# A gated linear recurrence on one Trainium2 core: keys and values of a head turned to tokens by VectorE instead of TensorE

## The reference

```python
def _gla_chunk(S, inp):
    q, k, v, logf = inp
    b = jnp.cumsum(logf, axis=2)
    ...                      # o: scores inside the chunk times v, plus q * exp(b) times S
    b_last = b[:, :, -1]
    S_new = jnp.exp(b_last)[..., None] * S + jnp.einsum(
        'bhck,bhcv->bhkv', k * jnp.exp(b_last[:, :, None] - b), v)
    return S_new, o
```

## Time and profile before

| | |
|---|---|
| median of 3 runs | 2688.05 us (2688.02 to 2688.28) |
| the profiled execution | 2687.86 us, span 2686.0 us |
| mean granted clock of TensorE | 0.998 of full |
| busy: TensorE, VectorE, ScalarE, POOL | 2656.1, 1764.7, 1300.7, 407.1 us |
| the recurrence's fourteen full trips | 440.63 us of the span |

### The profile page before, as it was taken

How to read it: one execution, slowest core, us unless ns; L and a number is a source line. 1 busy time by engine, 2 the same in 40 slices (tenths; PEclk the granted TensorE clock), 3 DMA queues, 4 the chain that set the end, 5 groups by cost and what they waited for, 6 DMA issues and landing times.

```text
span 2686.0 us, 55267 instructions
## 1 busy us (share of the span) xinstructions
PE 2656.1 (99%) x19742; PEld 2634.8 (98%) x19742; DVE 1764.7 (66%) x2908; ACT 1300.7 (48%) x2173; POOL 407.1 (15%) x792
## 2 busy tenths in 40 slices
PE   9999999999999999999999999999999999999997
PEld 9999999999999999999999999999999999999997
DVE  7888888848776534676645855548767535767644
ACT  6565666545444433444444566545444333444443
POOL 2111111101322100222200000002222101222200
PEclk9999999999999999999999999999999999999999
DMA  6444444444545555545555422344554555444553
GB/s 237 144 139 138 142 139 131 140 166 133 178 159 167 161 164 166 168 161 167 160 169 164 145 89 87 118 162 140 168 167 161 163 164 168 164 166 162 161 170 114
DMA packets 122673, 413.60 MB, mean 154 GB/s; under 512 B 13856, under 2 KB 20160, under 8 KB 122592
## 3 DMA queue, kind: packets, MB, share of 16 engines
q1 hardware_dynamic: 114480, 406.37, 47.0%
q10 hardware_dynamic: 7056, 3.21, 0.4%
q0 software_dynamic: 1056, 2.92, 0.3%
HBM read 406.97 MB, written 5.48 MB: 154 GB/s over the span
## 4 chain that ended last, share of the span: by engine, by line
PE 95%; DVE 4%; ACT 0%; issue 0%; DMA 0%; DVEq 0%; SPq 0%; ACTq 0%
PE bank L248 30%; PE bank L250 30%; PE bank L249 29%; DVE X L1163 1%; DVE Y L1160 1%; DVE h_lo L1147 1%; DVE w_lo L242 1%; PE bank L1718 1%; PE bank L828 1%; PE bank L789 1%; DVE Y L1177 1%; PE bank L796 0%; PE bank L829 0%; PE bank L1723 0%; ACT w_hi L235 0%
## 5 line engine op out<-in xcount | busy, mean ns | idle before, releaser
L248 PE MATMUL bank<-h_hi,w_hi 128*128 128x288 f32 (+1 forms) x4208 | 1262.1, 300 | 11.3 <-DVE h_lo L1147 8.4
L242 DVE TENSOR_TENSOR w_lo<-raw,w_hi 128x1024 fp32r<-128x1024 f32 (+1 forms) x784 | 952.3, 1225 | 451.8 <-ACT w_hi L235 451.4
L249 PE MATMUL bank<-h_lo,w_hi 128*128 128x288 f32 (+1 forms) x4208 | 1248.3, 297 | 0.0
L250 PE MATMUL bank<-h_hi,w_lo 128*128 128x288 f32 (+1 forms) x4208 | 1244.7, 296 | 0.0
L235 ACT ACTIVATE w_hi<-raw 128x1024 fp32r<-128x1024 f32 (+1 forms) x784 | 805.9, 1037 | 848.9 <-PE bank L250 843.0
L248 PEld LDWEIGHTS bank<-h_hi,w_hi 128*128 128x128 f32 x4208 | 788.8, 187 | 18.1 <-DVE h_lo L1147 11.4
L250 PEld LDWEIGHTS bank<-h_hi,w_lo 128*128 128x128 f32 x4208 | 792.3, 188 | 0.2
L249 PEld LDWEIGHTS bank<-h_lo,w_hi 128*128 128x128 f32 x4208 | 790.3, 188 | 0.6
L1332 POOL TENSOR_TENSOR ext<-yt,small 128x256 f32<-128x256 f32 x176 | 213.4, 1213 | 1500.8 <-ACT yt L1218 1034.7
L248 PE MATMUL bank<-g_hi,w_hi 128*128 128x288 f32 x1408 | 416.8, 296 | 0.0
L249 PE MATMUL bank<-g_lo,w_hi 128*128 128x288 f32 x1408 | 415.4, 295 | 0.0
(11 more groups left out here) (261 smaller groups left out, 2089.1 us busy)
## 6 DMA issues: line engine op xcount, KB each, us to landing
raw<-in_w_fi SPq DMA_DIRECT2D x352, 512.0 KB, 4.0
raw<-in_w_hi_in SPq DMA_DIRECT2D x128, 512.0 KB, 4.0
raw<-in_w_fo SPq DMA_DIRECT2D x128, 512.0 KB, 3.5
raw<-in_w_fo SPq DMA_DIRECT2D x64, 384.0 KB, 3.3
raw<-in_w_ho SPq DMA_DIRECT2D x32, 512.0 KB, 4.1
raw<-in_w_mo SPq DMA_DIRECT2D x32, 512.0 KB, 3.9
raw<-in_w_down SPq DMA_DIRECT2D x18, 512.0 KB, 4.1
raw<-in_w_ukv SPq DMA_DIRECT2D x16, 512.0 KB, 3.7
```

Of the source, the lines that this page charges most:

```text
L242: dve.tensor_tensor(lo, raw[:, ch.slot, 0:ch.units * P], hi.bitcast(F32), ALU.subtract).then_inc(lo_done, 1)
L248: pe.matmul(out, top[:, w], rhs_hi, start=start, stop=False)
L249: pe.matmul(out, top[:, w], rhs_lo, start=False, stop=False)
L250: return pe.matmul(out, rest[:, w], rhs_hi, start=False, stop=stop)
```

## The change

TensorE's transposes and ScalarE's copies of keys and values go. VectorE transposes blocks of 32 by 32 straight from `ke` to `ktok` and from `vfm` to `vtok`, 16 instructions for keys and 12 for values of a head, each on 32 partitions. A transpose of 32 by 32 blocks keeps each block's place, so a strip of 32 features and a part of 32 tokens go into one instruction that spans the blocks. In a full trip keys follow the masking of the scores, values follow the differences and the rest of the squares. `clamp` moves ahead of `lo(4)`. At the end of the recurrence keys of head t follow `scores_far`, and keys and values of head r follow `far_operands`. `updates` now waits for both; `values_out` on ScalarE waits for `v_tok` (VectorE) in place of `v_turned` (TensorE).

```diff
-                act.wait_ge(S["v_turned"], r)
+                act.wait_ge(S["v_tok"], r)
             act.activation(vfm[:], psum[2][:, 0:T], ACT.Copy).then_inc(evacuated, 1)
...
-        def keys_by_token(act, t):
-            act.wait_ge(S["k_turned"], t + 1)
-            act.activation(ktok[0:BL, 0:2, :], TR[0:BL, 0:2 * P], ACT.Copy)
-            act.activation(ktok[0:64, 2, :], TR[0:64, 2 * P:3 * P], ACT.Copy)
-            act.activation(ktok[64:BL, 3, :], TR[64:BL, 2 * P:3 * P], ACT.Copy).then_inc(S["k_tok"], 1)
...
-        def values_by_token(act, r):
-            act.wait_ge(S["v_turned"], r + 1)
-            act.activation(vtok[0:BL, :, :], TR[0:BL, 0:3 * P], ACT.Copy).then_inc(S["v_tok"], 1)
...
             if tail:
                 scores_near(dve, t)
                 scores_far(dve, t)
+                keys_by_token(dve, t)
+            if main:
+                clamp(dve, r)
             lo(4)
             if main:
-                clamp(dve, r)
                 gates_keys_queries(dve, r)
             lo(5)
...
             if tail:
                 squares_rest(dve, t)
+            if main:
+                values_by_token(dve, r)
             lo(7)
...
             scores_near(dve, t)
             gates_keys_queries(dve, r)
             scores_far(dve, t)
+            keys_by_token(dve, t)
             decay_sums(dve, r)
             lo(4)
             new_states(dve, t)
...
             decayed_keys(dve, r)
             near_operands(dve, r)
             far_operands(dve, r)
-            dve.wait_ge(S["o_raw"], t + 1)
+            keys_by_token(dve, r)
+            values_by_token(dve, r)
             decayed_queries(dve, r)
             out_scaled(dve, t)
             silu_gate(dve, r)
...
-        def turn_values(pe, r):
-            pe.wait_ge(S["scaled"], 4 * r + 3)
+        def keys_by_token(dve, t):
+
+            dve.wait_ge(S["ke_ready"], t + 1)
+            if past_first(t):
+                dve.wait_ge(S["updates"], t)
+            for q in range(P // 32):
+                cols = ke[32 * q:32 * q + 32, :].rearrange("p (b s m) -> p b s m", b=NB, m=32)
+                v = slice(32 * q, 32 * q + 32)
+                for i in range(SUBS - 1):
+                    dve.transpose(ktok[32 * i:32 * i + 32, 0:NB, v], cols[:, :, i, :])
+                dve.transpose(ktok[64:BL, 0:NB - 1, v], cols[:, 0:NB - 1, SUBS - 1, :])
+                z = dve.transpose(ktok[64:BL, NB, v], cols[:, NB - 1, SUBS - 1, :])
+            z.then_inc(S["k_tok"], 1)
+
+        def values_by_token(dve, r):
+
+            dve.wait_ge(S["scaled"], 4 * r + 3)
             if past_first(r):
-                pe.wait_ge(S["k_tok"], r)
-            for n in range(NB):
-                tr = pe.transpose(TR[0:BL, n * P:(n + 1) * P], vfm[:, n * BL:(n + 1) * BL], ident[:])
-            tr.then_inc(S["v_turned"], 1)
+                dve.wait_ge(S["o_raw"], r)
+            for q in range(P // 32):
+                cols = vfm[32 * q:32 * q + 32, :].rearrange("p (b s m) -> p b s m", b=NB, m=32)
+                for i in range(SUBS):
+                    z = dve.transpose(vtok[32 * i:32 * i + 32, :, 32 * q:32 * q + 32], cols[:, :, i, :])
+            z.then_inc(S["v_tok"], 1)
 
         def updates(pe, t, su=SU):
+            pe.wait_ge(S["v_tok"], t + 1)
+            pe.wait_ge(S["k_tok"], t + 1)
             for n in range(NB + 1):
...
-        def turn_keys(pe, r):
-            pe.wait_ge(S["ke_ready"], r + 1)
-            pe.wait_ge(S["v_tok"], r + 1)
-            for n in range(NB):
-                tr = pe.transpose(TR[0:BL, n * P:(n + 1) * P], ke[:, n * BL:(n + 1) * BL], ident[:])
-            tr.then_inc(S["k_turned"], 1)
...
                 pe.wait_ge(S["k_tok"], t + 1)
                 pe.wait_ge(S["att_ready"], t + 1)
                 updates(pe, t)
-            if main:
-                turn_values(pe, r)
             mm(3)
...
             mm(7)
             if main:
-                turn_keys(pe, r)
                 score_products(pe, r)
```

More of the change, by code:

```diff
@@ L380, in trunk_program @@
         names = ["scaled", "exps", "clamped", "logs", "sigmoids", "fgates", "queries", "gates", "logf", "decays", "ends_exp", "diffs",
-                 "diffs_exp", "odd_ready", "ke_ready", "pairs_ready", "v_turned", "v_tok", "k_turned", "k_tok", "levels_done",
+                 "diffs_exp", "odd_ready", "ke_ready", "pairs_ready", "v_tok", "k_tok", "levels_done",
                  "att_ready", "updates", "first_state", "second_state", "states", "zeroed", "o_raw", "o_squared", "o_sq_hi", "o_sq_lo", "o_summed", "o_logs", "o_rstd", "o_scaled",
@@ L515, in hgrn_act @@
                 gates_out(act, r)
-            if tail:
-                keys_by_token(act, t)
             hi(4)
@@ L531, in hgrn_act @@
             if main:
-                values_by_token(act, r)
                 decay_exps(act, r)
@@ L567, in hgrn_end_act @@
             state_load(act, r)
-            values_by_token(act, r)
             hi(6)
             out_root(act, t)
-            keys_by_token(act, r)
             out_top(act, t)
```

## The result

The changed kernel takes 2759.03 us (median of 5 runs, 2757.41 to 2762.49) against 2688.05 us before: a ratio of 1.0265, 95% interval 1.0253 to 1.0276. It is 71 us slower, where 42.5 us and at most 63 us more were forecast. The profiled execution took 2758.06 us, span 2756.2 us, so the spans differ by 70.2 us.

What follows compares the result with a forecast made beforehand. TensorE was taken as only just the bound, with VectorE's queue to bind afterwards. First trip +1.26, fourteen trips +33.6 and end +7.75 make +42.6 us on 2687.86: 2730.5 us, 1.6% slower, range 2698 to 2751.

Steps and rivals of the forecast that it cites:

- VectorE's queue: VectorE's in-order work and waits over one recurrence head: 31.42 us before, forecast 33.82 us and binding after the change.
- TensorE's floor: TensorE's own time per recurrence head: falls 0.66 us to 30.76 us, 10.6 us over sixteen heads if nothing else binds.
- 31.42 - 2.80 + X: VectorE's time per head: old length, minus waits given back, plus the 28 transposes' price, taken as 5.20 us.
- upper end of 0.14: Highest price for VectorE's transposes, no overlap: 0.14 us each over the elements, 6.32 us a head, 2748.4 us total.
- the three terms of the sum: First trip +1.26 us, fourteen full trips +33.6 us, end of the recurrence +7.75 us; together +42.6 us.
- The waits given back: VectorE's waits for ScalarE that the moves remove: 1.14 us by the clamp, 1.66 us by values, 2.80 us a head.
- the wait ahead of the last split: VectorE's 1.66 us wait per head for ScalarE's upper part; forecast to vanish because values' 2.40 us lie in it.
- Transposes that do not overlap, or worse: Rival on VectorE: each transpose starts only when the one before has written; 2748 us or above, chance 20%.
- The clock's fall: Rival: TensorE's clock falls in its new pauses; at two tenths, about 3 us a head, 2773 us; chance 4%.
- TensorE as the bound: Rival: transposes fit in VectorE's gaps, costing under 2.14 us a head; 10.6 us gained, 2677.3 us; chance 9%.
- The end: End of the recurrence, VectorE 93% busy: keys twice and values once, 8.00 us less 0.18 and 0.07, so +7.75 us.
- TensorE's share of the recurrence: Sign in the profile after: TensorE waits some 3 us in each of fourteen heads, its share falling to 91%.

Runs made afterwards that it cites:

- The series here: Kernel after plus seven series at VectorE's queue end, varying which partition quarter is read or written: 96-element transposes 0.28 us apart with changing quarters, 0.16 us with both fixed.
- the groups above: Kernel after plus 14 groups of four like instructions at VectorE's queue end: nine-block transposes 0.37 us apart, those with the change's strides 0.17 us on average.
- keys alone: Kernel after, but values stay with TensorE and ScalarE, so only keys are transposed on VectorE: 2740.47 us, ratio 1.0196.
- with the pause filled: Only keys transposed on VectorE, plus 8 useless TensorE products ahead of its wait for the states in each full trip: 2729.29 us, ratio 1.0153.
- values alone: Kernel after, but keys stay with TensorE and ScalarE, so only values are transposed on VectorE; clamp stays moved: 2699.06 us, ratio 1.004.
- nearly no transposes: Kernel after with 2 of a head's 28 transposes, all waits kept, results wrong: 2676.28 us, ratio 0.9955.
- filling the pauses: Kernel after with useless TensorE products in each full trip, 10 ahead of the wait for keys and 9 ahead of that for states: 2758.84 us, ratio 1.0262.

## Why the prediction was wrong

**The mechanism held.** VectorE's queue took the place of TensorE's floor, at 14 full trips, with the waits of 0.96, 0, 0.58 and 0.37 us that were left to it, and TensorE waits for VectorE in each. Of 31.42 - 2.80 + X the first two terms hold to 0.13 us: with the measured X of 7.04 it gives 35.66, measured 35.53. TensorE also waits ahead of the updates, which I had not said: I had keys ending 12.9 us after the trip's first split and TensorE arriving at 13.4; they end at 13.7 (239.22 to 252.90), and TensorE is there before. That was wrong at my own price too. At full clock TensorE gets from the outputs to the next updates in 26.7 us (259.46 to 288.56 - 2.39), so once the states release it (266.46 - 248.74 + 2.80 - 1.14 = 19.38 us after the first split), it arrives at 19.38 + 26.7 - 33.82 = 12.3 us into the next trip and not at the 13.4 of the old one. It did not touch the sum, since VectorE does not wait for these updates.

**The step that failed is X, the price of 28 instructions**, taken as 2.40 us of elements and 0.10 us for each. Measured: 2.40 + 4.64, so 0.166 us for each on the average, beyond even the upper end of 0.14. With 7.04 in place of 5.20 the three terms of the sum give 2.26 + 59.4 + 10.4 = 72.1 us, where the spans differ by 70.2. Nothing else is needed for the miss. The runs with one order changed price the instructions: 28 x 0.06 us, which is the shortest distance over the elements, and 24 x 0.12 us for the changes of quarter make 2.40 + 1.68 + 2.88 = 6.96 us of the 7.04.

What was wrong in it was the reading of two rows. L584 and L585 stood 0.17 and 0.21 us from their successors, and I averaged them to 0.107 us over their elements. They are two different cases: L585 follows L584 in the same quarter of partitions (96 elements, 0.10 + 0.07), and L586 goes to another (64 elements, 0.067 + 0.14: its predecessor's whole duration). Of the change's 28 instructions, 24 go to another quarter than the one before. The bound from above ("no overlap at all") was thus the usual case and not an extreme, and it was too low as well, since it took the duration of a copy: a transpose of 96 lasts 0.27 us, 0.167 over its elements, a copy 0.24 with PSUM as source. Of my two neighbouring rows one was the price.

The Trainium skill, VectorE: DVE Perf Modes, section "Two Vector instructions with no wait between them", has this rule: an instruction that starts in another quadrant than the last one that read or wrote the same memory is held until all earlier ones have finished. The series here agree, 0.28 us against 0.16 for transposes of 96 and 0.23 against 0.13 for copies. The prediction did not use it. The 311 ns for a transpose, from the section "The three transpose paths" of the same page of the Trainium skill, misled by little. The one element per cycle that the Trainium skill, Vector Engine (DVE) Microarchitecture Reference, section 3.8, states for the transposing array is confirmed by the groups above: transposes of 288 elements stand 0.37 us apart, 0.30 + 0.07.

**The waits given back** were right. Moving the clamp is worth 1.18 us a trip (36.71 against 35.53, forecast 1.14) where VectorE binds and next to nothing where TensorE does (2685.59). Values hide the wait ahead of the last split; keys alone leave its 1.65 us in place, which at 14 x 1.65 = 23 us is most of the difference between keys alone, 41 us with the pause filled, and values alone, 11.

**TensorE's floor** was right: 16 x 0.66 = 10.6 us forecast, 12.0 us measured with nearly no transposes. The clamp's 2.5 us are in that number; beside the kernel with only the clamp moved it is 2685.59 - 2676.28 = 9.3 us.

**The rivals.** "Transposes that do not overlap, or worse" was the true one, at 20%. Its second half has the size too: 0.026 us over its 0.14 for 28 x 14 instructions add 10 us to 2748. The stated range stopped at 2751 all the same. The clock's fall had 4% and is a real effect: 11 us with keys alone, but next to none in the kernel after, where filling the pauses changes one trip, by 0.6 us. TensorE as the bound needed 28 instructions in 2.14 us and was 4.9 us away.

**The end** was forecast as +7.75 and came to +10.7; keys twice and values once at the measured price, 10.68 - 0.25 = 10.4, account for it.

**Right by luck.** I had TensorE's share of the recurrence at 91%, and 91% was measured. But that share belonged to a trip of 33.82 us. In a trip of 35.53 us a floor of 30.76 us is 87%, and that is what the trips at full clock show:

```profile
430.55:466.07 35.52, 31.02 (x234) 30.58 (x234) 32.56 (x88) 17.93 (x32) 5.15 (x4) 1.00 0.38 124
```

In the ten others the mean granted clock is 0.91 or 0.95, and TensorE is busy for 32.5 to 33.9 us with the same products. The lower clock filled the pause up to the forecast share.

## What to carry to other kernels

When VectorE takes over work in many small instructions on 32 partitions, price each by whether it reads and writes the same quarter of partitions as the one before: if not, count its predecessor's whole duration. Look in the trace for a pair of each kind before averaging neighbouring rows.

An engine that is 83% busy in a queue of fixed order is not 17% free: add the work up from start to start, ask of each wait whether the new work can lie in it, and compare the sum with the other engine's floor. Where an engine is only just not the bound, moving one instruction ahead of a wait is worth its full time after the change and next to nothing before it.

Here values lay in a wait and keys did not. Keys stand ahead of the clamp, and a wait of 0.96 us for what ScalarE makes of the clamp stays in every trip. With the clamp ahead of keys as well, keys could lie in it; ScalarE had by then waited for the clamp (5.64 us in the trip shown). By these rows that could be worth up to 14 x 0.96 = 13 us, an estimate: no run tried that order.

If TensorE pauses in each trip, look at the granted clock behind the pause before explaining a trip's length by waits alone.

## What the runs showed of the hardware

A change of quarter, read or written, makes the next VectorE instruction wait for the end of the one before: transposes of 96 elements 0.28 us apart against 0.16 to 0.17, copies 0.23 against 0.13. By that rule no order within the values' series can remove it, since each of its twelve instructions needs another pair; the two orders tried take the same 3.37 us.

A pause of TensorE of 1.8 us was followed by a stretch at a lower clock (0.60 on the average over 4 us) in six trips of keys alone and not in six others with the same pause; useless products in the pause took 11 us off the kernel. What decides between the two kinds of trip was not found.
